# Replacing stage barriers by own end signals and moving modulation slab pairs in a two-layer diffusion trunk

## The reference

```python
def layer(x, cond, p, l, angles, ctx):
    mod = jax.nn.silu(cond) @ p['w_mod'][l] + p['b_mod'][l]
    sh1, sc1, g1, sh2, sc2, g2 = jnp.split(mod, 6, axis=-1)
    h = rms_norm(x, p['norm1'][l]) * (1.0 + sc1) + sh1
    mixed, ctx_out = token_mixers(h, p, l, angles, ctx)     # GQA, gated linear attention, differential attention,
    x = x + g1 * mixed                                      # each with w_branch, sigmoid gates, then w_out
    h = rms_norm(x, p['norm2'][l]) * (1.0 + sc2) + sh2
    a, u = jnp.split(h @ p['w_ffn_in'][l], 2, axis=-1)
    x = x + g2 * ((jax.nn.silu(a) * u) @ p['w_ffn_out'][l])
    return x, ctx_out
```

## Time and profile before

| what | value |
|---|---|
| median of 3 executions | 2383.72 us (2383.45 to 2384.16) |
| the profiled execution | 2385.3 us |
| its span, first to last instruction | 2383.5 us |
| mean granted TensorE clock | 0.992 of full |
| layer 0 / layer 1, first to last matmul: `project_attention` | 197.98 to 318.40 / 1372.86 to 1493.76 |
| `attention` | 319.35 to 454.60 / 1494.70 to 1626.00 |
| `merge` | 458.03 to 717.32 / 1628.19 to 1887.49 |

### The profile page before, as it was taken

One profiled execution on the slowest core, in us unless ns is written; L12 is line 12 of the kernel. 1 busy time (PEld: TensorE's weight loads), 2 busy tenths in 40 slices (PEclk: granted clock), 3 DMA queues, 4 the chain that ended last, 5 costly groups with the idle time before them and its releaser, 6 DMA issues. The chain is left out here.

```text
span 2383.5 us, 40526 instructions
## 1 busy us (share of the span) xinstructions
PE 2311.7 (97%) x16311; PEld 2140.5 (90%) x16311; DVE 1497.3 (63%) x2403; ACT 1065.8 (45%) x2121; POOL 190.6 (8%) x160
## 2 busy tenths in 40 slices
PE   7999999899999999999999999999999999999999
PEld 6877877799999999999987777778999999999998
DVE  5445568676665865747643564787666668467473
ACT  5523357644443642524345333774444345244252
POOL 1430000100003000000215200000000110000000
PEclk9999999999999999999999999999999999999999
DMA  9225440122225222322231163102222422323222
GB/s 297 98 68 172 143 152 28 45 80 80 81 89 159 71 79 81 89 89 72 89 125 53 51 207 112 33 1 71 80 81 80 165 75 78 100 66 95 68 70 84
DMA packets 246665, 224.01 MB, mean 94 GB/s; under 512 B 6944, under 2 KB 232304, under 8 KB 245968
## 3 DMA queue, kind: packets, MB, share of 16 engines
q1 hardware_dynamic: 242528, 219.25, 29.6%
q0 software_dynamic: 480, 0.66, 0.3%
q10 hardware_dynamic: 3472, 1.52, 0.2%
HBM read 211.70 MB, written 9.70 MB: 93 GB/s over the span
## 5 line engine op out<-in xcount | busy, mean ns | idle before, releaser
L2356 ACT ACTIVATE ring_high<-raw 128x512 fp32r<-128x512 f32 (+1 forms) x278 | 158.1, 609 | 250.5 <-PE ps L2710 149.8
L2496 DVE TENSOR_TENSOR ring_low<-raw,ring_high 128x512 fp32r<-128x512 f32 (+1 forms) x278 | 204.4, 761 | 70.4 <-ACT ring_high L2356 66.2
L2775 PE MATMUL ps<-hH,ring_low 128*128 128x320 f32 x640 | 198.0, 309 | 0.5 <-ACT f_r L2400 0.2
L2775 PE MATMUL ps<-hH,ring_high 128*128 128x320 f32 x640 | 197.8, 309 | 0.0
L2775 PE MATMUL ps<-hL,ring_high 128*128 128x320 f32 x640 | 197.7, 309 | 0.0
L1564 DVE SCALAR_TENSOR_TENSOR xT<-ps,mod,xT 128x512 f32<-128x512 f32 (+1 forms) x128 | 64.0, 545 | 192.7 <-PE ps L2710 192.7
L359 PE MATMUL ps<-wH,hL 128*128 128x512 f32 (+1 forms) x460 | 177.1, 385 | 5.2 <-DVE wL L871 2.6
L359 PE MATMUL ps<-wH,hH 128*128 128x512 f32 (+1 forms) x460 | 171.6, 373 | 0.0
L2710 PE MATMUL ps<-gH,ring_low 128*128 128x320 f32 x704 | 160.8, 310 | 0.3 <-DVE xT L1564 0.3
L2710 PE MATMUL ps<-gH,ring_high 128*128 128x320 f32 x704 | 160.5, 309 | 0.0
L2710 PE MATMUL ps<-gL,ring_high 128*128 128x320 f32 x704 | 160.4, 309 | 0.0
(11 more groups left out here) (384 smaller groups left out, 6192.3 us busy)
## 6 DMA issues: line engine op xcount, KB each, us to landing
raw<-in_w_in SPq DMA_DIRECT2D x56, 1024.0 KB, 5.3
raw<-in_w_ffn_in SPq DMA_DIRECT2D x88, 512.0 KB, 5.2
gmod<-in_w_mod SPq DMA_DIRECT2D x24, 1024.0 KB, 8.6
raw<-in_w_ffn_out SPq DMA_DIRECT2D x16, 1024.0 KB, 5.1
b_raw<-in_w_branch SPq DMA_DIRECT2D x22, 512.0 KB, 4.4
head_w<-in_w_mod SPq DMA_DIRECT2D x8, 1024.0 KB, 12.5
modw<-in_w_mod SPq DMA_DIRECT2D x8, 1024.0 KB, 7.6
raw<-in_w_out SPq DMA_DIRECT2D x8, 1024.0 KB, 5.9
```

Source lines behind the costliest of these rows:

```text
L2356: nc.scalar.activation(ring_block(m.ring_high, b, src.shape[1], src.shape[2]), src, ACT.Copy).then_inc(m.sem("w_high"), 1)
L2496: nc.vector.tensor_tensor(ring_block(m.ring_low, b, nk, cols), src, ring_block(m.ring_high, b, nk, cols).bitcast(F32), ALU.subtract).then_ ...
L2775: last = nc.tensor.matmul(m.ps[:, plan.banks[n, 0][BANK[what]], 0:HALF], w[:, k, :], a[:, k, :], start=(first and k == 0 and q == 0), stop ...
```

## The change

Three things are changed.

1. All stages are written into one block, `m.whole`. The barrier between stages is replaced by `border()`: GpSimd, ACT and DVE each drain and raise a semaphore of their own (`ended`); SP waits for the stage's last matmul (`last_matmul`) and raises its own; each of these four waits for the other three, PE waits for GpSimd, DVE and ACT alone and is not drained. GpSimd then clears the semaphores. At the end of the program all semaphores are cleared and a second barrier is added.
2. In `project_attention` the first pair moves from after tile 1 to after tile 4 of slab 2. In layer 1 the stage takes slabs 8 to 15 only (four pairs), and loads slabs 16 and 17 for the attention.
3. `attention` of layer 1 takes slabs 16 to 19 as two pairs. In both layers the first pair stands at the start and the last pair after all other matmuls of the stage. Layer 0: pairs at the start, in steps 4 and 10, and at the end; transposes in steps 5 (two rows) and 11 (one row). Layer 1: one at the start, its transpose in step 2, one at the end. Loads that fitted two by two behind used buffers are issued earlier, into other buffers. The last pair is finished in `merge`: ACT copies its row before its first other work, PE transposes it after the first gate tile, DVE sums it, adds the bias and makes `affine` after its two `difference`s, at (g, what) = (0, 1); PE waits for the bias (`late_added`) before `branch(0, 1)`, which takes the bank.

```diff
+    def border(self):
+        self.stage += 1
+        k, ended = self.stage, self.ended
+        matmuls, count = self.sem(self.last_matmul[0]), self.last_matmul[1]
...
+        @self.whole.sync
+        def _(sp):
+            sp.wait_ge(matmuls, count)
+            sp.sem_inc(ended["sp"], 1)
+            for engine in ("pool", "dve", "act"):
+                sp.wait_ge(ended[engine], k)
+        @self.whole.gpsimd
+        def _(pool):
+            pool.drain().then_inc(ended["pool"], 1)
+            for engine in ("dve", "act", "sp"):
+                pool.wait_ge(ended[engine], k)
+            self.clear(used)
...
+        @self.whole.vector
+        def _(dve):
+            dve.drain().then_inc(ended["dve"], 1)
+            for engine in ("pool", "act", "sp"):
+                dve.wait_ge(ended[engine], k)
+        @self.whole.tensor
+        def _(pe):
+            for engine in ("pool", "dve", "act"):
+                pe.wait_ge(ended[engine], k)
...
+def attention_mods(L):
+    return [(L + 1, slab) for slab in (0, 2, 4, 6)] if L + 1 < DEPTH else [(L, 16), (L, 18)]
...
 def project_attention(nc, m, d, L):
-    mods = range(8, 20)
-    mod_at = {(2 + q, 1): (2 * q, 2 * q + 1) for q in range(len(mods) // 2)}
+    mods = range(8, 20 if more else 16)
+    mod_at = {(2 + q, 1 if q else 4): (2 * q, 2 * q + 1) for q in range(len(mods) // 2)}
...
 def attention(nc, m, d, L, nxt):
-    pairs = 4 if more else 0
-    mod_at = {6 * p - 2: p for p in range(1, pairs)}
-    turn_at = {6 * p - 1: p // 2 for p in range(1, pairs, 2)}
+    pairs = attention_mods(L)
+    buffers = [(0, 1), (2, 3), (4, 5), (4, 5)] if more else [(0, 1), (4, 5)]
+    mod_at = {4: 1, 10: 2} if more else {}
+    turn_at = {5: (0, 1), 11: (2,)} if more else {2: (0,)}
...
+            for p in ((1, 2) if more else (1,)):
+                load_pair(p)
+            store_values(sp)
             for j in range(2):
-                next_load(sp, m, nxt, j, *(("slab_used", 2 * pairs - 3 + j) if more else ()))
+                next_load(sp, m, nxt, j, "slab_used", 2)
+            if more:
+                sp.wait_ge(m.sem("slab_used"), 6)
+                load_pair(3)
...
+            pe.wait_ge(*freed(len(chunks) - 2))
+            mod_pair(len(pairs) - 1, len(chunks))
...
-            order.step(affine(nc, m, dve, order, L, 1))
             if more:
-                dve.wait_ge(*freed(max(turn_chunk.values())))
-                order.step(affine(nc, m, dve, order, L + 1, 0))
+                order.step(affine(nc, m, dve, order, L, 1))
...
 def merge(nc, m, d, L, nxt, late_bank):
             act.sem_inc(m.sem("w_high"), 4)
+            nc.scalar.activation(m.late_row[:, :], m.ps[:, late_bank, 0:W256], ACT.Copy).then_inc(m.sem("late_row"), 1)
...
+                    if g == 0 and what == 1:
+                        layer, slab = attention_mods(L)[-1]
+                        dve.wait_ge(m.sem("late_turned"), 1)
+                        summed_late = order.step(sum_mod(nc, m, late_bank, W256, 2, 2))
+                        dve.wait_ge(*summed_late)
+                        add_mod_bias(nc, m, layer, 2 * slab, 2).then_inc(m.sem("late_added"), 1)
+                        dve.wait_ge(m.sem("late_added"), 1)
+                        order.step(affine(nc, m, dve, order, layer, 0 if layer > L else 1))
...
+                        if (g, c) == (0, 0):
+                            pe.wait_ge(m.sem("late_row"), 1)
+                            turn_mod(nc, m, m.late_row, late_bank, W256).then_inc(m.sem("late_turned"), 1)
                     for c in range(2):
+                        if (g, c) == (0, 1):
+                            pe.wait_ge(m.sem("late_added"), 1)
                         branch(g, c).then_inc(m.sem("tile_done"), 1)
...
 def program(nc, d):
-        head(nc, m, d)
-        for L in range(DEPTH):
+        with nc.Block() as m.whole:
+            head(nc, m, d)
+            for L in range(DEPTH):
...
+        m.clear([s.num for used in m.sem_sets for s in used] + [s.num for s in m.ended.values()])
+        nc.all_engine_barrier()
         nc.all_engine_barrier()
```

More of the change, by code:

```diff
@@ L972, in _ @@
                                  m.kv[:, 8, CTX, :]).then_inc(m.sem("k_stored0"), 16)
-            for j in (10, 11):
+            for j in range(10, len(mods)):
                 sp.wait_ge(m.sem("mod_used"), j - 1)
                 load_mod(j)
[L976 to L980, removed]
+            sp.wait_ge(m.sem("low_ready"), n)
+            layer, slab = attention_mods(L)[0]
+            for j in range(2):
+                sp.dma_start(m.modw[j][:, :, :], k_tiles(d["w_mod"], layer, (slab + j) * W256, W256)
+                             ).then_inc(m.sem(f"attention_mod{j}"), 16)
             for h in range(2):
@@ L987, in _ @@
             sp.wait_ge(m.sem("caches"), 6 * 16)
-            if more:
-                for j in range(2):
-                    sp.wait_ge(m.sem(f"attention_mod{j}"), 16)
+            for j in range(2):
+                sp.wait_ge(m.sem(f"attention_mod{j}"), 16)
         @block.scalar
@@ L1268, in store_values, with load_pair @@
                              m.kv[:, 4:8, CTX, :]).then_inc(m.sem("v_stored"), 16)
[L1270 to L1280, removed]
+            def load_pair(p):
+                layer, slab = pairs[p]
+                for i, b in enumerate(buffers[p]):
+                    sp.dma_start(m.modw[b][:, :, :], k_tiles(d["w_mod"], layer, (slab + i) * W256, W256)
+                                 ).then_inc(m.sem(f"mod_loaded{b}"), 16)
+            for b in buffers[0]:
+                sp.sem_inc(m.sem(f"mod_loaded{b}"), 16)
+            for p in ((1, 2) if more else (1,)):
+                load_pair(p)
+            store_values(sp)
             for j in range(2):
-                next_load(sp, m, nxt, j, *(("slab_used", 2 * pairs - 3 + j) if more else ()))
+                next_load(sp, m, nxt, j, "slab_used", 2)
+            if more:
+                sp.wait_ge(m.sem("slab_used"), 6)
+                load_pair(3)
             next_loaded(sp, m, nxt)
@@ L1349, in mod_pair @@
             def mod_pair(p, c):
[L1350 to L1353, removed]
+                for i, b in enumerate(buffers[p]):
+                    pe.wait_ge(m.sem(f"mod_loaded{b}"), 16 * sum(b in x for x in buffers[:p + 1]))
+                    mod_groups(nc, m, m.modw[b], 6 + c % 2, i).then_inc(m.sem("slab_used"), 1)
             for c in first_mods:
@@ L1374, in _ @@
                     if turn is not None:
-                        pe.wait_ge(*freed(mod_chunk[2 * turn + 1]))
-                        for i in range(2):
-                            last = turn_mod(nc, m, m.mrow[:, 2 * turn + i, :], 6 + c % 2, i * W256)
+                        pe.wait_ge(*freed(mod_chunk[turn[-1]]))
+                        for i, p in enumerate(turn):
+                            last = turn_mod(nc, m, m.mrow[:, p, :], 6 + c % 2, i * W256)
                     if mod is not None:
@@ L1539, in _ @@
                         if turn is not None:
-                            done = order.step(sum_mod(nc, m, 6 + c % 2, 0, 4, 2))
+                            done = order.step(sum_mod(nc, m, 6 + c % 2, 0, 2 * len(turn), 2))
                             dve.wait_ge(*done)
-                            for i in range(2):
-                                ins = add_mod_bias(nc, m, L + 1, 8 * turn + 4 * i, 2, 8 * i)
+                            for i, p in enumerate(turn):
+                                ins = add_mod_bias(nc, m, pairs[p][0], 2 * pairs[p][1], 2, 8 * i)
                         if n:
@@ L1751, in head @@
     order8 = [0, 4, 1, 5, 2, 6, 3, 7]
-    tiles, z_tiles, _, _, bank, before = number_tiles(slabs, {})
+    tiles, z_tiles, _, total, bank, before = number_tiles(slabs, {})
     lr_copied = tiles[1][0] + 1
+    m.last_matmul = "tile_done", total
     with m.block() as block:
```

51 lines of the change are left out of this document (35 added, 16 removed).

## The result

The changed kernel takes 2394.3 us (median of 5 runs, 2391.6 to 2397.8), the kernel before 2384.2 us (2383.5 to 2386.3). The ratio is 1.0043, with a 95% interval of 1.0032 to 1.0053. The change makes the kernel slower. The forecast was 2383.1 us, in a range of 2378.5 to 2388.0. The profiled execution took 2394.3 us with a span of 2392.5 us, 9.0 us more than the span before.

What follows compares the result with a forecast made beforehand. PE, busy for 2311.7 of 2383.5 us, was taken as the bound. The terms -1.5 + 0.2 - 4.7 - 3.9 - 3.0 + 12.3 sum to -0.6 us, giving 2383.1 us as median, range 2378.5 to 2388.

Steps and rivals of the forecast that it cites:

- own signals, ten borders: Stage borders: end signals in place of barriers save 0.15 us each, -1.5 us in all (0 to -3.1).
- end of the program: Program end: the added clearing and barrier cost one more crossing, +0.2 us.
- first pair later: Projections of both layers: PE's wait for the first pair's slab loads goes, with no new wait, -4.7 us.
- two pairs fewer in layer 1: Layer 1's projection, bound by PE: two pairs less of PE time, -3.9 us.
- attention 0: Layer 0's attention: one pair and one row leave the inside, -2.3 us.
- attention 1: Layer 1's attention: a first pair fills PE's idle time (-1.04), one row is added (+0.33), -0.7 us.
- last pair: End of each attention: its 1.93 us fit PE's idle 3.43 us (layer 1: 2.19), so it costs nothing.
- merges: Both merges: PE stalls 5.9 us for DVE's late sum, then 1.65 us of slow clock; +12.3 us in two layers.
- rival A: Merge: no stall before `branch(0, 1)`, merges give -2.7 instead of +12.3, time 2368.1 us; chance 0.08.
- rival B: Projections: the slab wait moves to the second pair, up to 6.3 us in each layer, time 2395.7; chance 0.06.
- Rival C: Attention and borders: the attention gives nothing back and the signals nothing, +4.5 us, time 2387.6; chance 0.10.

Runs made afterwards that it cites:

- e2: The changed kernel with the barriers of the kernel before put back between its stages, all else as changed: 2394.6 us.
- e8: The kernel before with the own end signals in place of the barriers and nothing else changed: 2385.2 us, ratio 1.0002.
- e4: The kernel before with only the first pair of projection slabs taken after tile 4 instead of tile 1: 2379.7 us, ratio 0.9980.
- e3: The changed kernel with the two key stores ahead of the two loads for the attention in SyncE's queue: 2390.4 us, ratio 1.0023.
- e1: The changed kernel with DVE's late block in the merge moved ahead of the splits of the second gate slab: 2378.3 us, ratio 0.9970.
- e7: The changed kernel with late block early, stores first, barriers back, and each attention's single turned row moved behind the last pair: 2371.2 us, ratio 0.9943.
- e6: The changed kernel with three edits: late block early, key stores ahead of the loads, barriers back: 2373.0 us, ratio 0.9951.

## Why the prediction was wrong

| step | forecast | measured | from |
|---|---|---|---|
| own signals, ten borders | -1.5 | +0.4 | e2 against changed |
| end of the program | +0.2 | +0.7 | e2, e8 |
| first pair later | -4.7 | -4.5 | e4 against before |
| two pairs fewer in layer 1 | -3.9 | -3.9 | e3 against e4: 115.17 - 119.11 |
| key store behind two loads | 0 | +4.2 | changed: 2.5 of waiting, 1.7 of clock; gone in e3 |
| attention 0 | -2.3 | -1.6 | changed, e2 |
| attention 1 | -0.7 | +1.0, and +1.6 of clock | e2 against e4 and e8, changed |
| last pair | 0 | 0.0 | below |
| merges | +12.3 | +14.2 | changed |

The row of attention 1 counts from a profile before without its low stretch (132.4 us, e4 and e8). The measured terms exceed the forecast's by 1.9 + 0.5 + 0.2 + 4.2 + 0.7 + 1.7 + 1.6 + 1.9 = 12.7 us. Less the 1.05 us of low clock in the profile before, and less the 2.2 us of the stages that the change leaves alone, 9.4 us remain; the span missed the forecast by 9.0 + 0.6 = 9.6. So the time left the range by several misses of one sign, of which the key store is the largest. With that wait removed, e3 still takes 2390.4 us, above the range.

**The merge: mechanism right, size a little low.** `late_added` at 23.7 us after the merge's first matmul was forecast and came at 23.7 in layer 0; the wait is 5.6 us there (forecast 5.9) and 6.4 in layer 1, whose ACT met its gate slab later. The term that was too small is the clock behind the stall. I took one stretch of 3.4 us; it was 6.8 us, of which some 4.3 fell on running matmuls, so it cost 2.2 us in layer 0 (in layer 1, where it began 1.7 us before the stall's end, 2.6) instead of 1.65. e1 shows that the whole stall was the place of DVE's block. The cover that I named for the last pair exists: from DVE's last maximum of the attention to the merge's first matmul it is 13.51 us with the pair (e2) and 13.52 without (e4) in layer 0, 12.31 and 12.28 in layer 1. Where I wrote of the late chain that none of it depends on PE, I had DVE's idle time ahead of its third low part before me and did not draw the conclusion that the time of rival A was one move away.

**The step that failed: the projection of layer 1.** The forecast priced the two pairs that leave it, rightly, and overlooked what comes in: two loads of 1 MB on SyncE's queue, ahead of a store that ACT's next copy waits for. It names neither the loads nor the store. PE came 3.9 us sooner to this place as well, so that the store's delay could no longer hide. In layer 0 the same order costs little, since PE is later there by two pairs: e3 gains 0.65 us in it at most. The delay could have been read before the change, in layer 0 of the kernel before, where the same store takes 7.4 us. Of -8.6 us forecast for both projections -3.6 are left: 4.2 went into this wait and its clock, the rest into small waits at the second pair (0.41 and 0.25 us, where rival B had 6.3 in each layer) and at the borders. This alone, put into the sum, gives 2387.3 us, still inside the range.

**The signals.** The middle of the bounds was the wrong choice, and the upper bound of the cost was missing: I bounded it by 0, and a border can get dearer, 0.06 to 0.19 us where ACT ends the stage. Rival C had this half right.

**Attention.** The row's price was read as PE's time of two transposes, 0.33 us. A single row's chunk cost 0.97 and 0.99 us (e7 against e6), over my upper bound of 0.7, since a chunk also takes a turn of the two banks. In layer 0 the number of row chunks stays at two: the one with two rows in step 17 goes and one with a single row comes in step 11, so the gain is 2.61 less 1.01, that is 1.6 us. And the gain of 1.04 us in layer 1 was no property of the kernel: e4 and e8, with the same attention code as before, lack the low stretch and with it this microsecond. I had compared two layers of one execution in which one had a low stretch and the other had none. That the changed kernel's profile then had a low stretch there after all adds 1.6 us, and I can't say why it fell there.

The clock rule that I cited from the Trainium skill (TensorE: Matmul & The Clock Gate, Part 1) says that the number of slow matmuls varies between runs. The traces agree that it varies: behind the six stalls of the merge (changed, e2, e3) the low clock lay on running matmuls for 3.5 to 5.9 us, and so cost 1.7 to 2.9 us. These costs lie at or above my 1.65 us, and none is near the 0.7 us that I worked out from that page's figures.

**Open.** The low stretches that come in some executions only stay unexplained: which execution has one in the GLA stage, at an attention's start or in a tail was not found from anything in the profiles. They cost 1.0 to 1.7 us each, and the runs of one kernel spread by 3 to 7 us. The six stalls of the merge in three traces (changed, e2, e3) each go with 6.8 us of low clock, the wait of some 2.5 us in layer 1's projection with 3.4 us in two traces (changed, e2) and with none in e1; why was not tested. The changed kernel's trace at step 11 shows the wait for the bank in layer 0 alone; that the same wait makes the 0.99 us of layer 1 is argued from the equal price.

## What to carry over

When a part of a change adds transfers to a queue, list what stands behind them in the queue and who waits for that, before pricing what they replace; and when it lets an engine arrive earlier, look at what it will meet there. A small step on a strictly ordered engine costs what its place costs: four instructions of 0.2 us in each merge stalled TensorE for 12 us in all, and the same four, moved up by 16 us into idle time, stalled it no more. Before one layer's time is used to price another's, check that the granted clock is the same in both.

## What was not expected of the hardware

The granted clock fell to 0.50 for 3.4 us in some executions of the same code and not in others. In the GLA stage of layer 0 (before, e3, e6, e8) it fell within 0.2 us of the end of a wait of PE of 1.35 us, and the other five executions have this wait at full clock. At an attention's start (changed, e1, e3) no wait just before was over 0.82 us, and in the tails (e1, e3, e7) none in the 10 us before was over 0.4 us. In e1, for example, layer 0's attention lasts 138.61 us with this window in it, and 137.03 us in e2 without:

```profile
326.20:329.60 3.40, 3.40 (x19) 2.34 (x19) 2.20 (x4) 1.37 (x5) 0.00 (x0) 0.50 1.11 344
```

At the six stalls of 5.5 to 6.5 us it was low for 6.8 us each time, from within the stall. A store of 128 KB landed after 7.4 to 7.5 us behind two loads of 1 MB, and after 1.8 to 1.9 us ahead of them.
